# Key latents normed before they are halved, keys taken out by ScalarE, and short products set between long ones

## The chip, the cores and the metric

The kernel runs on one core of a Trainium2 chip. Its engines are TensorE (PE in the profile, with its weight loads as PEld), VectorE (DVE), ScalarE (ACT), GpSimd (POOL) and SyncE (SP), which here issues every DMA. Each engine runs its own instructions strictly in the order in which they were written, and waits on semaphores. The metric is the device time of one execution in microseconds, as the median of several.

## What is computed

Two transformer blocks on 512 tokens of width 1024, all in float32 with the token axis along the free dimension. The second block, where the change lies, has two attentions side by side:

```python
h = rmsnorm_2(x, norm_g[l])
(q_lat, c_kv, k_rope, z_a, q_b, k_b, v_b, z_b,
 q_idx, k_idx, w_idx, gate_a, gate_b) = jnp.split(h @ w_in[l], cuts, axis=-1)
q = (rmsnorm_2(q_lat, g_q_lat[l]) @ w_uq[l])      # 384 latents -> 8 heads of 96
kv = (rmsnorm_2(c_kv, g_kv_lat[l]) @ w_ukv[l])    # 256 latents -> 8 heads of 64 keys + 64 values
...
y_a = mla_attention(q_nope, q_pe, k_nope, k_pe, v_a, pos) * silu(z_a)
y_b = dsa_attention(q_b, k_b, v_b, q_idx, k_idx, w_idx, rel_bias, pos, topk) * silu(z_b)
merged = sigmoid(gate_a) * (y_a @ w_o_a[l]) + sigmoid(gate_b) * (y_b @ w_o_b[l])
x = x + merged @ w_out[l]
```

The second attention (dsa) first scores all keys with eight small index heads, keeps the 128 best keys of each query, and masks the rest.

## The kernel before

**Products.** Every product of float32 matrices is made of three passes: each operand is split in a high half, a rounded copy that ScalarE makes, and a low half, the remainder that VectorE or GpSimd subtracts (`HH`/`HL` for the normed input, `LQH`/`LQL` for the query latents, `LKH`/`LKL` for the key latents, `WH`/`WL` for weights). The three matmuls of a tile are lines 1352 to 1354, of 512 columns each. Weights come in units of 8 tiles: SyncE loads a unit into `WS` (L1235) once the low half of the unit three before it is made, ScalarE makes `WH` (L1537), GpSimd in this part of the program makes `WL` (L2115), and a unit is asked for two units ahead of its use. A `product` of eight tiles thus takes 24 matmuls in four quarters of six, and ends in a take-out of its PSUM bank. Products use bank 0 and bank 1 in turn (`d_ring`), so a product can start only when the take-out of the product but one before it is done.

**Order.** Nothing is scheduled at run time. Python generators write one list of steps; `weave` takes one step of the main work and then so many of the side work, a product giving way after each quarter, and every engine follows the list.

**Index stage.** The main work is `index_scores` (24 index products, L1502, into four banks in turn; ScalarE turns each into `i_t`, L1731; VectorE adds it into `score`, L2026 and L2029). The 24 come as three blocks of eight heads, for 512, 384 and 256 columns. The side work is `latents`, then `mla_v`, then `mla_products(0)`:
- `latents` makes the key latents `ckv0`, `ckv1` and the query latents `ql0` to `ql2`. A latent (`lat_out`) is taken out by VectorE into a buffer `tmp` (L2049), squared by ScalarE (L1545), added up by GpSimd into `acc` (L2163), split by ScalarE (L1735) and VectorE (L2054). The sums over the partitions are matmuls with ones (L1383, and L1389 for the same sums token by token). After `ql0` the key sums are turned into the norm `RK` and, token by token, into `rtok` (step `norm_kv`: Ln, Ln, Exp, Exp with two table loads, L1739 to L1747). After three quarters of `za0`, the first gate product, the query sums follow, and `norm_q` makes `RQ` (L1750 to L2058).
- `mla_v` is the value product, four token blocks of twelve short matmuls (L1376 to L1378), taken out by ScalarE with the scale `rtok` into `a_v` (L1563).
- `mla_products(p)` is, for a pair of heads, the key product `uk` (2 tiles), the two query products `uq` (3 tiles each) and, past the first pair, `za` (8 tiles). VectorE takes the keys out times `RK` (step `mla_k`, L2062, two instructions of 64 rows) and the queries times `RQ` (`mla_q`, L2065).

**Attention stage.** The main work is the attention of eight mla heads and then eight dsa heads. Per head it has four blocks: logits (L1456, or L1461 to L1467 for dsa), row maximum on VectorE (L1922, or L1926 for dsa), exponential on ScalarE (L1635), scaling by the inverse sum (L1640 on ScalarE, for dsa L1937 on VectorE), transposes (L1475) and the product with the values (L1484). The side work is `mla_side`, which holds the remaining products in a fixed order. VectorE also finds the 128 best keys in 48 rounds of two scans (L2038, L2040). Each dsa head needs stacked halves of its queries and keys (`dsa_stack`); four DMAs for a pair of heads (L1283, L1288) move rows, and stand in SyncE's queue between the weight loads.

## Time and profile before

| | us |
|---|---|
| median of 3 runs | 1107.36 |
| range of the runs | 1106.17 to 1107.45 |
| the profiled execution, its own time | 1106.37 |
| its span in the profile | 1104.6 |
| PE busy in it | 1050.1 |
| DVE / ACT / POOL busy | 623.3 / 469.3 / 256.6 |

The span is the time from the first to the last recorded instruction of the profiled execution. PE is busy for 95% of it; what a change can gain or lose is mostly found in PE's remaining 54.5 us, each of them a wait for another engine or for a DMA. In the timeline a row gives the start and the duration of an instruction or of several merged ones, and in brackets how long the engine stood idle before it and on whom it waited.

### The profile page before, as it was taken

To read this page: it belongs to the slowest core of one execution; us is meant where nothing else is said; L and a number is where in the kernel's file an instruction comes from. 1 tells how busy PE (TensorE), PEld (TensorE's weight loads), DVE (VectorE), ACT (ScalarE), POOL (GpSimd) and SP (SyncE) were. 2 spreads that over 40 slices of the span, in tenths; PEclk is the share of its full clock that TensorE was granted. 3 is DMA by queue.
4 is the path that set the end of the run, shared out by engine and by line. 5 is a ranking of instruction groups with operands and counts; after the bars stand their busy time and mean duration, and the time that the engine had idled before them with its cause. 6 is when DMAs were issued, how large, how long until landed. Compare 5 with 4: busy or idle time off the path is not lost.

```text
span 1104.6 us, 13494 instructions
## 1 busy us (share of the span) xinstructions
PE 1050.1 (95%) x5160; PEld 843.1 (76%) x5160; DVE 623.3 (56%) x1048; ACT 469.3 (42%) x815; POOL 256.6 (23%) x155
## 2 busy tenths in 40 slices
PE   7799889899999999999999998799999999999996
PEld 5597677667888888888888776577787766788885
DVE  6755577747454433344444556898756665425544
ACT  6634346546322222132334465545764554423322
POOL 0581332222101000011113323422323223321100
PEclk9999899999999999999999999999999999999998
DMA  8031132212223232223233326212222423122222
GB/s 293 4 122 50 39 117 78 78 58 77 96 96 96 98 131 77 94 83 109 93 100 94 110 70 209 85 39 74 60 88 78 118 91 104 59 96 96 99 73 77
DMA packets 34655, 102.32 MB, mean 93 GB/s; under 512 B 4544, under 2 KB 8016, under 8 KB 34592
## 3 DMA queue, kind: packets, MB, share of 16 engines
q1 hardware_dynamic: 34592, 101.47, 28.3%
q8 instruction: 41, 0.67, 0.3%
q14 instruction: 22, 0.18, 0.1%
HBM read 93.35 MB, written 4.74 MB: 89 GB/s over the span
## 4 chain that ended last, share of the span: by engine, by line
PE 73%; DVE 14%; ACT 6%; issue 4%; SPq 2%; DMA 1%; DVEq 0%; POOL 0%; ACTq 0%; POOLq 0%
PE bank L1352 20%; PE bank L1354 20%; PE bank L1353 20%; PE bank L1484 2%; PE bank L1475 2%; PE bank L1364 1%; DVE m L2038 1%; DVE score L2029 1%; PE bank L1366 1%; PE bank L1365 1%; DVE score L2040 1%; ACT WH L1537 1%; DVE f_s L1828 1%; DVE small L1922 1%; PE bank L1456 1%
## 5 line engine op out<-in xcount | busy, mean ns | idle before, releaser
L1352 PE MATMUL bank<-HH,WH 128*128 128x512 f32 x808 | 330.1, 409 | 16.9 <-DVE WL L1784 8.3
L1354 PE MATMUL bank<-HH,WL 128*128 128x512 f32 x808 | 317.8, 393 | 0.0
L1353 PE MATMUL bank<-HL,WH 128*128 128x512 f32 x808 | 317.4, 393 | 0.0
L2115 POOL TENSOR_TENSOR WL<-WS,WH 128x1024 fp32r<-128x1024 f32 x64 | 154.8, 2419 | 358.1 <-ACT WH L1537 357.7
L1352 PEld LDWEIGHTS bank<-HH,WH 128*128 128x128 f32 x808 | 154.2, 191 | 54.4 <-DVE WL L1784 8.3
L1537 ACT ACTIVATE WH<-WS 128x1024 fp32r<-128x1024 f32 x162 | 168.6, 1047 | 56.5 <-PE bank L1354 41.5
L1354 PEld LDWEIGHTS bank<-HH,WL 128*128 128x128 f32 x808 | 153.1, 189 | 33.4
L1353 PEld LDWEIGHTS bank<-HL,WH 128*128 128x128 f32 x808 | 153.8, 190 | 29.5 <-issue 1.0
L1784 DVE TENSOR_TENSOR WL<-WS,WH 128x1024 fp32r<-128x1024 f32 x98 | 130.3, 1335 | 25.9 <-ACT WH L1537 25.9
L2168 POOL TENSOR_TENSOR fa<-fa,fg 128x512 f32<-128x512 f32 x22 | 28.3, 1285 | 273.4 <-DVE fa L1975 273.4
L1352 PE MATMUL bank<-GH,WH 128*128 128x512 f32 x176 | 68.5, 389 | 0.0
L1353 PE MATMUL bank<-GL,WH 128*128 128x512 f32 x176 | 68.5, 389 | 0.0
L1354 PE MATMUL bank<-GH,WL 128*128 128x512 f32 x176 | 68.5, 389 | 0.0
L1955 DVE TENSOR_TENSOR X<-X,bank 128x512 f32<-128x512 f32 x39 | 26.7, 685 | 67.9 <-PE bank L1354 67.8
L1680 ACT ACTIVATE GH<-fa 128x512 fp32r<-128x512 f32 x22 | 13.9, 632 | 114.3 <-POOL fa L2168 114.3
L1545 ACT ACTIVATE sq<-X 128x512 f32<-128x512 f32 x31 | 19.5, 629 | 74.5 <-DVE X L1955 74.2
L1364 PE MATMUL bank<-WH,HH 128*128 128x256 f32 x160 | 47.2, 295 | 2.0 <-ACT f_v L1563 2.0
L1648 ACT ACTIVATE PT<-bank 128x128 f32<-128x128 f32 (+1 forms) x96 | 41.1, 428 | 16.1 <-PE bank L1475 15.9
L1366 PE MATMUL bank<-WH,HL 128*128 128x256 f32 x160 | 45.2, 283 | 0.0
L1365 PE MATMUL bank<-WL,HH 128*128 128x256 f32 x160 | 45.2, 283 | 0.0
L1977 DVE TENSOR_TENSOR GL<-fa,GH 128x512 fp32r<-128x512 f32 x22 | 15.2, 692 | 46.8 <-ACT GH L1680 46.8
L1676 ACT ACTIVATE fs<-fg 128x512 f32<-128x512 f32 x22 | 13.9, 632 | 59.6 <-DVE fg L1966 59.6
(339 smaller groups left out, 1749.7 us busy)
## 6 DMA issues: line engine op xcount, KB each, us to landing
WS<-wall SPq DMA_DIRECT2D x162, 512.0 KB, 3.4
scratch<-rows SPq DMA_DIRECT2D x8, 320.0 KB, 5.6
X<-xT SPq DMA_DIRECT2D x8, 256.0 KB, 6.2
b_t<-scratch SPq DMA_DIRECT2D x8, 256.0 KB, 3.8
outT<-X SPq DMA_DIRECT2D x8, 256.0 KB, 2.1
b_m<-b_m SPq DMA_DIRECT2D x11, 128.0 KB, 4.1
f_s<-f_s SPq DMA_DIRECT2D x8, 128.0 KB
f_m<-f_m SPq DMA_DIRECT2D x8, 128.0 KB
```

What stands on the lines that cost most here:

```text
L1352: e.matmul(b[:, :], wh, xh[:, at_k, :], start=k == 0, stop=False)
L1353: e.matmul(b[:, :], wh, xl[:, at_k, :], start=False, stop=False)
L1354: m = e.matmul(b[:, :], wl, xh[:, at_k, :], start=False, stop=k == n - 1)
L1364: e.matmul(b[:, 0:256], xh[:, k, cs], wh, start=k == 0, stop=False)
L1365: e.matmul(b[:, 0:256], xh[:, k, cs], wl, start=False, stop=False)
L1366: m = e.matmul(b[:, 0:256], xl[:, k, cs], wh, start=False, stop=k == NK - 1)
L1537: e.activation(WH[:, u % NW, :], WS[:, u % NST, :], ACT.Copy).then_inc(*w_hi.tick(u))
L1648: e.activation(dst, s["b"][:, 0:128 * i + 128].rearrange("p (a n) -> p a n", n=128), ACT.Copy).then_inc(*moved.tick(s["u"]))
L1784: e.tensor_tensor(WL[:, u % NW, :], WS[:, u % NST, :], f32(WH[:, u % NW, :]), ALU.subtract).then_inc(*w_low_v.tick(u))
L1955: e.tensor_tensor(X[:, m, :], X[:, m, :], s["b"][:, :], ALU.add).then_inc(*out_v.tick(s["name"]))
L2115: e.tensor_tensor(WL[:, u % NW, :], WS[:, u % NST, :], f32(WH[:, u % NW, :]), ALU.subtract).then_inc(*tick(w_low_g, u))
L2168: e.tensor_tensor(a[:, :], a[:, :], fg[jj % 3][:, :], ALU.mult).then_inc(*tick(gate_up, jj))
```

## The change

It has five parts.
- **Latents of the keys.** `ckv0` and `ckv1` are taken out into `a_q[2]` and `a_q[3]`. They are not split at once: after `ql2` two new VectorE steps multiply them by `RK` (`norm_latent`), and only then they are split.
- **Sums.** The key sums and `norm_kv` stand after `ql1` and not after `ql0`. The token-by-token sums (four matmuls with one column) and their two small activations are gone, since the values no longer need a scale.
- **Keys.** The keys are taken out by ScalarE with a plain copy, not by VectorE; the logits wait for ScalarE as well.
- **Order in the first pair.** The four blocks of the value product alternate with `uk0`, `uq0` and `uq1`.
- **Order in the attention stage.** `mla_side` puts `za`, a part of `dsa_products(0)` or a gate product between the short `uk` and `uq` products. The gate product `gate_a(1)` moves for that from the dsa part to the mla part.

```diff
@@ lat_out
+                if x == "lk":
+                    do("latent", c=c, x=x, name=name, b=b, t=a_q[2 + c], free=None)
+                    add_square((x, c), total_g, a_q[2 + c][:, :], None, out_v(name))
+                    return out_v(name)
@@ latents
-                if c == 0:
+                if c == 1:
                     i1, b1 = column_sums("lk", acc[1], total_g(("lk", 1)))
-                    i2, b2 = token_sums("lkt", [acc[1]], total_g(("lk", 1)))
-                    do("norm_kv", b1=b1, b2=b2)
+                    do("norm_kv", b1=b1)
                     t_ring.give(i1, norm_a("lk ln"))
-                    t_ring.give(i2, norm_a("lkt ln"))
+                if c == 2:
+                    for c2 in range(2):
+                        do("norm_latent", c=c2, t=a_q[2 + c2])
+                        do("halve_latent", c=c2, x="lk", t=a_q[2 + c2])
+                        known.add(("lk", c2))
@@ the first pair
+        def first_pair():
+            values = mla_v()
+            for part in (mla_key(0), lambda: mla_query(0, 0), lambda: mla_query(0, 1)):
+                next(values)
+                yield
+                yield from part() if callable(part) else part
+            yield from values
@@
-        side = chain(latents(), mla_v(), mla_products(0))
+        side = chain(latents(), first_pair())
@@ mla_side
-            yield from mla_products(1)
-            yield from dsa_products(0)
-            yield from mla_products(2)
-            yield from gate_a(0)
-            yield from mla_products(3)
+            yield from mla_key(1)
+            yield from z_products("za", P_ZA, 1)
+            yield from mla_query(1, 0)
+            yield from dsa_query(0)
+            yield from mla_query(1, 1)
+            yield from dsa_key(0)
+            for p in range(2, 4):
+                yield from mla_key(p)
+                yield from gate_a(p - 2)
+                yield from mla_query(p, 0)
+                yield from z_products("za", P_ZA, p)
+                yield from mla_query(p, 1)
...
-            yield from gate_a(1)
@@ scalar_program
+                elif kind == "mla_k":
+                    r = slice(64 * s["hl"], 64 * s["hl"] + 64)
+                    q.wait_ge(dense(f"uk{s['p']}"), s["free"])
+                    e.activation(s["dst"][0:64, :], s["b"][r, :], ACT.Copy).then_inc(*out_a.tick(s["name"]))
@@ vector_program
-                elif kind == "mla_k":
...
+                elif kind == "norm_latent":
+                    q.wait_ge(norm_a("lk"), square(("lk", s["c"])))
+                    e.tensor_tensor(s["t"][:, :], s["t"][:, :], RK[:, :], ALU.mult).then_inc(*norm_v.tick(("lk", s["c"])))
```

Three places show how the order moves. The first is ScalarE's queue around `norm_kv` (`RK` and `rtok`). Before, it stood behind the last `i_t` of `ql0`'s stretch and ahead of the split `WH` and the `i_t` of head 4 of the first block:

```order
L1731 ACTIVATE i_t3_159<-bank7 128x512
L1739 ACT_TABLE_LOAD
L1739 ACTIVATE RK_214<-bank5,eps_61 128x512
L1742 ACTIVATE rtok_64<-bank4,eps_61 128x4
L1745 ACT_TABLE_LOAD
L1745 ACTIVATE RK_214<-RK_214 128x512
L1747 ACTIVATE rtok_64<-rtok_64 128x4
L1537 ACTIVATE WH_53<-WS_52 128x1024
L1731 ACTIVATE i_t0_156<-bank2 128x512
```

Now it stands behind the last `i_t` of the first block and ahead of the next split and of the first `i_t` of the second block (384 columns). The seven instructions between the two places (a split, four `i_t`, a square and a split of a latent) are as before.

```order
L1766 ACTIVATE LQH_162<-tmp1_70,V_60 128x512
L1762 ACTIVATE i_t3_159<-bank7 128x512
L1770 ACT_TABLE_LOAD
L1770 ACTIVATE RK_214<-bank5,eps_61 128x512
L1773 ACT_TABLE_LOAD
L1773 ACTIVATE RK_214<-RK_214 128x512
L1568 ACTIVATE WH_53<-WS_52 128x1024
L1762 ACTIVATE i_t0_156<-bank2 128x384
L1762 ACTIVATE i_t1_157<-bank6 128x384
```

The second place is one product further on, after `ql2`. ScalarE has before, ahead of `RQ`:

```order
L1545 ACTIVATE sq1_68<-tmp0_69 128x512
L1735 ACTIVATE LQH_162<-tmp0_69,V_60 128x512
L1731 ACTIVATE i_t3_159<-bank7 128x384
L1537 ACTIVATE WH_53<-WS_52 128x1024
L1731 ACTIVATE i_t0_156<-bank2 128x384
L1731 ACTIVATE i_t1_157<-bank6 128x384
L1750 ACT_TABLE_LOAD
L1750 ACTIVATE RQ_213<-bank5,eps_61 128x512
```

and now the two splits of the key latents, each of which waits for VectorE's multiplication, stand ahead of `WH`:

```order
L1576 ACTIVATE sq1_68<-tmp0_69 128x512
L1766 ACTIVATE LQH_162<-tmp0_69,V_60 128x512
L1762 ACTIVATE i_t3_159<-bank7 128x384
L1766 ACTIVATE LKH_164<-a_q2_187,V_60 128x512
L1766 ACTIVATE LKH_164<-a_q3_188,V_60 128x512
L1568 ACTIVATE WH_53<-WS_52 128x1024
L1762 ACTIVATE i_t0_156<-bank2 128x384
L1762 ACTIVATE i_t1_157<-bank6 128x384
L1780 ACT_TABLE_LOAD
L1780 ACTIVATE RQ_213<-bank4,eps_61 128x512
```

VectorE's queue at that place, now; before, the third row was followed at once by the fourth and the ninth:

```order
L2059 SCALAR_TENSOR_TENSOR score_160<-i_t2_158,wi_72,score_160 128x384
L2079 TENSOR_TENSOR tmp0_69<-bank0,Rb_62 128x512
L2084 SCALAR_TENSOR_TENSOR LQL_163<-tmp0_69,V_60,LQH_162 128x512
L2059 SCALAR_TENSOR_TENSOR score_160<-i_t3_159,wi_72,score_160 128x384
L2091 TENSOR_TENSOR a_q2_187<-a_q2_187,RK_214 128x512
L2084 SCALAR_TENSOR_TENSOR LKL_165<-a_q2_187,V_60,LKH_164 128x512
L2091 TENSOR_TENSOR a_q3_188<-a_q3_188,RK_214 128x512
L2084 SCALAR_TENSOR_TENSOR LKL_165<-a_q3_188,V_60,LKH_164 128x512
L2059 SCALAR_TENSOR_TENSOR score_160<-i_t0_156,wi_72,score_160 128x384
```

Four instructions more are on VectorE between the query latent and the next scores (the two `LKL` splits stood earlier before). The third place is TensorE's queue after the first block of the value product and the first index product of the third block (256 columns). Before, the second value block followed, in bank 1:

```order
L1378 MATMUL bank0<-WH_53,LKL_165 128x256
L1502 MATMUL bank2<-i_kk_145,i_qq0_148 128x256
L1376 MATMUL bank1<-WH_53,LKH_164 128x256
L1377 MATMUL bank1<-WL_54,LKH_164 128x256
L1378 MATMUL bank1<-WH_53,LKL_165 128x256
```

Now the first pair's key product stands there, also in bank 1:

```order
L1409 MATMUL bank0<-WH_53,LKL_165 128x256
L1533 MATMUL bank2<-i_kk_145,i_qq0_148 128x256
L1383 MATMUL bank1<-LKH_164,WH_53 128x512
L1384 MATMUL bank1<-LKL_165,WH_53 128x512
L1385 MATMUL bank1<-LKH_164,WL_54 128x512
```

Bank 1 holds `za0` until its take-out in both.

## Rows read from the trace of the kernel before

**Rows 1.** Part 1 of the page: busy us, share of the span, instructions.
```profile
PE 1050.1 (95%) x5160; PEld 843.1 (76%) x5160; DVE 623.3 (56%) x1048; ACT 469.3 (42%) x815; POOL 256.6 (23%) x155
```

**Rows 2.** Whom TensorE waited for, 640 to 800 us: total, times, longest.
```profile
PE bank L1383 <- POOL acc L2163: 4.4, 1, 4.4
PE bank L1352 <- DVE a_q L2065: 4.3, 2, 3.1
PE bank L1376 <- DVE zb L1801: 1.6, 1, 1.6
PE bank L1475 <- ACT Pc L1640: 1.0, 1, 1.0
...
PE bank L1376 <- ACT a_v L1563: 0.4, 1, 0.4
```

**Rows 3.** The same view, 720 to 1000 us.
```profile
PE bank L1461 <- issue: 2.2, 1, 2.2
PE bank L1461 <- DVE sq_late L2001: 1.7, 1, 1.7
```

**Rows 4.** TensorE's timeline: start, duration, what, idle time before.
```profile
667.22 1.02 PE L1383 MATMUL bank<-acc,ones 128*128 128x512 f32 x2
668.08 0.95 PE L1389 MATMUL bank<-ones,acc 128*128 128x1 f32 x8
...
682.53 0.44 PE L1502 MATMUL bank<-i_kk,i_qq 96*128 96x384 f32 x1 [0.74 <-ACT i_t L1731]
...
691.84 2.07 PE L1383 MATMUL bank<-acc,ones 128*128 128x512 f32 x2 [4.39 <-POOL acc L2163]
...
699.45 0.39 PE L1376 MATMUL bank<-WH,LKH 128*128 128x256 f32 x1 [1.65 <-DVE zb L1801]
...
716.96 0.50 PE L1352 MATMUL bank<-LQH,WH 128*128 128x512 f32 x1 [3.07 <-DVE a_q L2065]
```

**Rows 5.** Chain of work: the weight load that ScalarE waits for.
```profile
670.36 3.87 DMA WS<-wall
```

**Rows 6.** ScalarE's timeline.
```profile
669.65 1.28 ACT L1739 ACT_TABLE_LOAD   x1
...
673.64 0.19 ACT L1747 ACTIVATE rtok<-rtok 128x4 f32<-128x4 f32 x1
674.25 1.06 ACT L1537 ACTIVATE WH<-WS 128x1024 fp32r<-128x1024 f32 x1 [0.42 <-DMA WS<-wall]
...
683.32 1.24 ACT L1731 ACTIVATE i_t<-bank 128x384 f32<-128x384 f32 x3
...
690.29 0.71 ACT L1735 ACTIVATE LQH<-tmp,V 128x512 fp32r<-128x512 f32 x1
...
691.27 1.04 ACT L1537 ACTIVATE WH<-WS 128x1024 fp32r<-128x1024 f32 x1
...
696.39 0.63 ACT L1753 ACTIVATE RQ<-RQ 128x512 f32<-128x512 f32 x1
...
880.13 0.62 ACT L1713 ACTIVATE b_s<-b_st 64x512 fp32r<-64x512 f32 x1
```

**Rows 7.** VectorE's timeline.
```profile
675.82 4.29 DVE L2029 SCALAR_TENSOR_TENSOR score<-i_t,wi,score 128x512 f32<-128x512 f32 x3 [5.22 <-ACT i_t L1731]
...
684.11 2.37 DVE L2026 TENSOR_SCALAR score<-i_t,wi 128x384 f32<-128x384 f32 x1
...
689.04 0.68 DVE L2049 TENSOR_TENSOR tmp<-bank,Rb 128x512 f32<-128x512 f32 x1
...
691.03 1.31 DVE L2054 SCALAR_TENSOR_TENSOR LQL<-tmp,V,LQH 128x512 fp32r<-128x512 f32 x1 [1.31 <-ACT LQH L1735]
...
698.71 0.68 DVE L1801 SCALAR_TENSOR_TENSOR zb<-bank,Rb 128x512 f32<-128x512 f32 x1
```

**Rows 8.** GpSimd's timeline: one low half of a weight unit.
```profile
683.57 2.69 POOL L2115 TENSOR_TENSOR WL<-WS,WH 128x1024 fp32r<-128x1024 f32 x1 [0.78 <-ACT WH L1537]
```

**Rows 9.** 692 to 696 us: length, PE, PEld, DVE, ACT, POOL busy, clock, DMA share, GB/s.
```profile
692.00:696.00 4.00, 4.00 (x10) 2.60 (x11) 3.90 (x4) 3.95 (x6) 2.63 (x1) 0.61 0.00 0
```

**Rows 10.** SyncE's timeline around the DMAs of head 6.
```profile
913.58 5.54 SPq L1235 DMA_DIRECT2D WS<-wall  x2
919.17 0.47 SPq L1283 DMA_DIRECT2D b_m<-b_m  x1
919.68 0.59 SPq L1288 DMA_DIRECT2D b_m<-b_m  x1
```

More of the change, by code:

```diff
@@ L937, in out @@
                 add_square((x, c), total_g, t[:, :], None, out_v(name))
-                do("halve_latent", c=c, x=x, t=t, name=name)
+                do("halve_latent", c=c, x=x, t=t)
                 tmp_ring.give(m, low((x, c)))
@@ L977, in mla_v @@
                 do("mm_av", tb=tb, tiles=tiles, b=b, free=free)
-                do("out_tok", name="av", tb=tb, dst=a_v[:, tb, :], b=b, scale=rtok[:, 4 + tb:5 + tb],
-                   norm=norm_a("lkt"), free=[index_in[0](), index_in[1]()])
+                do("out_tok", name="av", tb=tb, dst=a_v[:, tb, :], b=b, scale=1.0, norm=None,
+                   free=[index_in[0](), index_in[1]()])
                 d_ring.give(i, out_a(("av", tb)))
@@ L995, in z_products, with mla_key @@
             gates[name] = i, z
-        def mla_products(p):
+        slots_of = {}
+        def mla_key(p):
             while not aq_ring.ready(2):
                 yield "not yet"
-            slots = [aq_ring.take() for _ in range(2)]
+            slots = slots_of[p] = [aq_ring.take() for _ in range(2)]
             def k_out(b):
@@ L1004, in k_out, with mla_query, out @@
                     do("mla_k", name=(f"uk{p}", hl), hl=hl, dst=a_k[slots[hl][0]], p=p, b=b, free=slots[hl][2])
-                return out_v((f"uk{p}", 1))
-            def q_out(hd, hl):
-                def out(b):
-                    do("mla_q", name=f"uq{hd}", dst=a_q[slots[hl][0]], b=b, free=slots[hl][2])
-                    known.add(f"uq{hd}")
-                    return out_v(f"uq{hd}")
-                return out
-            yield from product(f"uk{p}", "w_ukv_2", 0, cols(256 * p, 64) + cols(256 * p + 128, 64), "lk", 2, k_out)
-            for hl in range(2):
-                hd = 2 * p + hl
-                yield from product(f"uq{hd}", "w_uq_2", 0, cols(96 * hd, 96) + cols(96 * hd + 80, 16)
-                                   + cols(96 * hd + 64, 16), "lq", 3, q_out(hd, hl))
-            if p:
-                yield from z_products("za", P_ZA, p)
-            mla_in[p] = slots
+                return out_a((f"uk{p}", 1))
+            yield from product(f"uk{p}", "w_ukv_2", 0, cols(256 * p, 64) + cols(256 * p + 128, 64), "lk", 2, k_out)
+        def mla_query(p, hl):
+            hd, slot = 2 * p + hl, slots_of[p][hl]
+            def out(b):
+                do("mla_q", name=f"uq{hd}", dst=a_q[slot[0]], b=b, free=slot[2])
+                known.add(f"uq{hd}")
+                return out_v(f"uq{hd}")
+            yield from product(f"uq{hd}", "w_uq_2", 0, cols(96 * hd, 96) + cols(96 * hd + 80, 16)
+                               + cols(96 * hd + 64, 16), "lq", 3, out)
+            if hl:
+                mla_in[p] = slots_of[p]
+        def first_pair():
[5 more added lines that the diff above has]
+            yield from values
         def mla_pair(p):
@@ L1086, in dsa_stack, with dsa_query @@
                 yield
-        def dsa_products(p):
+        dsa_free = {}
+        def dsa_query(p):
             while (p == 1 and ("logits", ("mla", 5, 3)) not in known) or (p == 2 and ("logits", ("mla", 7, 3)) not in known) \
@@ L1099, in dsa_products @@
             first.append(dsa_stack(p))
+        def dsa_products(p):
+            yield from dsa_query(p)
+            yield from dsa_key(p)
         def dsa_pair(p):
@@ L1454, in tensor_program @@
                     elif kind == "logits_mla":
-                        q.wait_ge(out_v(f"uq{hd}"), rope("end"), keys_in(), s["free"])
+                        q.wait_ge(out_v(f"uq{hd}"), out_a((f"uk{hd // 2}", hl)), rope("end"), keys_in(), s["free"])
                         e.matmul(b[:, 0:n], s["qk"][0][:, qs], s["qk"][1][:, 0:n], start=True, stop=False)
```

16 lines of the change are left out of this document (5 added, 11 removed).

## The prediction

> **What bounds the kernel now.** The first view is the page's part 1: TensorE is busy 1050.1 us of a span of 1104.6 [rows 1], so it is the bound, and a change counts by how it shortens TensorE's work or its waits. The second is the table of TensorE's waits. In the stretch that the change rewrites it lists one wait of 4.4 us for GpSimd's sum of squares, 4.3 us for two query take-outs, 1.6 and 0.4 us in the value product and 1.0 us in the attention [rows 2]; behind it 2.2 and 1.7 us at the first logits of two dsa heads [rows 3]. The third is the timeline of each engine, which says what stands behind such a wait. The 4.39 us ahead of 691.84 [rows 4] end with a GpSimd addition, but that is the end of a chain: VectorE takes `ql2` out at 689.04, because it was busy with scores before that, and one score there lasted 2.37 us [rows 7], while GpSimd held a weight split from 683.57 for 2.69 us [rows 8]. ScalarE then needs 0.71 us for each split copy [rows 6]. So between 667 and 717 us the small engines, with their queues in fixed order, set the pace, and what counts there is which instruction stands ahead of which. A loss comes on top: after the 4.39 us the granted clock is 0.61 over the next 4 us [rows 9], part of them at the lower level of 1.2 GHz; the stretch shows what a long wait costs beyond itself.
>
> **The change part by part.** All times are those of the profiled execution; I follow the queues with its durations.
>
> *Sums, TensorE's side.* The token sums go: from 668.08 to the next product at about 668.9 [rows 4] is 0.8 us, and `ql1` starts 1.7 us earlier since the other sums now follow it. This is worth nothing yet. ScalarE's split at 674.25 waits for a weight load that SyncE issued at 670.36 [rows 5, 6], behind DMAs the change leaves alone. VectorE's three scores start at 675.82 behind it [rows 7], `ql1` is taken out after them, and the index product at 682.53 waits for the `i_t` at the end of that chain [rows 4]. TensorE arrives there 0.8 us earlier and waits 0.8 us longer: 0.
>
> *`norm_kv`, ScalarE's side.* Before, it ran from 669.65 to 673.83 [rows 6], in time in which ScalarE would have waited for that load anyway: it cost nothing. Now the cover is gone. It stands at 682.4, ahead of a weight split and the first `i_t` of the second block. Without the two small activations it is two table loads of 1.28 us, an Ln of 0.7 and an Exp of 0.6, 3.9 us. That `i_t`, the first of three from 683.32 [rows 6], ends at 687.7, and the score that ran at 684.11 [rows 7] starts then: **+3.6**. Everything queued behind it on VectorE shifts with it: the take-out of `ql2` to 692.7, the query sums on TensorE from 691.84 to 695.5. Meanwhile TensorE waits at index product 4 of the second block for the same `i_t` (about 3.6 us) and at the sums again (about 4.6). The two are one delay of 3.6 over the wait of before.
>
> *Latents normed late.* One latent costs a multiplication (0.65), ScalarE's copy (0.71), VectorE's remainder (0.7), none overlapping the next, since each engine waits for the other. The nearest row is the query latent, where VectorE stands 1.31 us for ScalarE and its own part then takes 1.31 against GpSimd [rows 7]. After `LQL` at 696.0 and a score, the first key latent is ready at 698.7, the second at 700.7. TensorE reaches the value product at 699.6 and waits about a microsecond for the second. That is small. What matters is who is queued behind: ScalarE's `WH`, before at 691.27 [rows 6], stands behind both splits and starts at 699.9, **+8.6**. From there to the end of `RQ` it is 691.27 to 697.0, 5.75 us [rows 6]: `RQ` is ready at 705.65. VectorE then has its `RQ` product, a score and the take-out of `za0`, which ends at 707.6; before it ran at 698.71 [rows 7]. `za0` holds bank 1. TensorE has by then done the first value block and one index product, and waits for bank 1 from 702 on; before it continued at 699.45 [rows 4]. It is **8.2 us late** at 707.6.
>
> *The first pair.* From 699.45 to 716.96 [rows 4] TensorE did the other three value blocks, `uk0`, `uq0`, `uq1`, `uk1` and seven index products. Without its waits (0.4 and 4.3 [rows 2]) that is 17.5 - 4.7 = 12.8 us, and the same work stands there now, in another order. The long waits for `uq` take-outs go, as the value blocks stand between. New ones come: ScalarE has, after 707.6, a tanh, a split, a value take-out, an `i_t`, a second split, and only then the two keys (priced at the 64-row copy of 0.62 [rows 6]), so `uq0` starts at 712.2, about a microsecond late; two GpSimd splits in a row slow the scores ahead of `uq0`'s take-out, so `uq1` starts at 717.4, 1.3 us late; and the clock after the wait for bank 1 falls as in [rows 9], partly hidden in these waits. `uk1` ends at 722.65 where before it was over by 716.96: **+5.7** so far. Bounds: 3 (the new waits do not occur) to 9 (they each cost a score under GpSimd, 2.4, more).
>
> *Keys on ScalarE.* Eight instructions of some 0.7 us leave VectorE, which is full in the attention's first 30 us. The logits' new wait is met long before, as other products stand between. Of the 1.0 us wait of the transposes [rows 2] and two of 0.2 next to it I take 0.7 as gained; bounds 0 and 1.3, and 2 lost if ScalarE, with keys ahead of an exponential, becomes late instead. **-0.7**.
>
> *`gate_a(1)` moved.* It leaves the dsa part, so the last query and key products come 5.6 us of TensorE's time earlier. Head 6's DMAs were issued at 919.17 and 919.68 behind a weight load that SyncE held until 919.1 [rows 10], and its logits waited 2.2 us [rows 3]. In the new order one weight load fewer stands between and the stack is made one block of the attention, some 3.5 us, earlier: the wait goes, **-2.2**. Head 4's wait of 1.7 [rows 3] keeps its order, but its weight split stands behind one more PT copy: **+0.5**. Elsewhere in that part the same instructions stand in nearly the same order.
>
> Sum: 5.7 - 0.7 - 2.2 + 0.5 = **+3.3 us**. On the profiled execution this is 1106.37 + 3.3 = 1109.7. That execution is 1.0 us below the median, whose runs spread over 1.3; on the median it is 1107.36 + 3.3 = 1110.7, which I forecast.
>
> The scores that stretch under GpSimd's splits are a term of this sum. The row of 2.37 us against 0.6 shows it. The Trainium skill (SBUF — State Buffer, the section on ports) gives the rule: VectorE with two inputs in SBUF and GpSimd hold one port pair in turn, each for a whole instruction, so the one that starts first wins. By that rule the new multiplications by `RK` can also be held up, by up to one split; in my timing they fall between two splits. A second place speaks harder against the change: the Trainium skill (ScalarE: Activation LUTs, What ACT_TABLE_LOAD costs) prices a table switch at about 2.66 us with a drain. The row has 1.28 us, and two loads with all four activations fit between 669.65 and 673.83 [rows 6]. By the page's figure the sum would be 2.8 us higher; I go by the row.
>
> **The rivals.**
> *A: the change does what its parts suggest.* `norm_kv` and the late norm find cover, since ScalarE is only 42% busy [rows 1]; then the token sums' 0.8, the waits of 4.3 and 0.4, the 1.0 and the 2.2 go, 8.7 us together: 1098.7. For it speaks the idle time of ScalarE in the stretch. Against it: that idle time lies where ScalarE waits for VectorE to take a latent out, and the new place is between two such waits, right where VectorE's next score hangs on ScalarE. The point from which it decides is 684.11: if the score of that row starts before 685, A is right.
> *B: slower at first, given back later.* The delay up to `uk1` is there but nearer its lower bound of 3 us, and the attention, relieved on VectorE, and the two dsa heads give back 3.9: within 1 us of before, 1107.
> *C: the small engines stay late.* VectorE reaches the attention with its scans still to do, and ScalarE has the keys besides; two or three more waits of 1 to 2 us in the attention, and clock drops after each long wait: 3.3 + 5 = 1115.7.
> *D: the new order does not reach the waits.* If bank waits and not the queues decided, the interleaving would change nothing past 0.8 us: 1106.6. The rows give each wait a queue, so this is weak, and is counted with B.
>
> **How the numbers follow.** Forecast 0.52, A 0.15, B and D 0.20, C 0.13. A measurement tells 0.2%, 2.2 us, from no change. Forecast and C, less the edge of the forecast below +2.2 (0.07), give slower 0.58; that edge and most of B give same 0.24; A and a little of B give faster 0.18. The range leaves out the far part of A and the far part of C: from 1102.5, a gain of half of A, to 1115. The likeliest case's own range is 1108.5 to 1113.5.
>
> **What would show it.** Right, in the profile of after: the first score of the second block near 687.7 and not 684; TensorE waiting at an index product of 384 columns for `i_t` for over 3 us, then at the query sums for over 4; a wait of some 5 us of `uk0` for `za0`'s take-out near 707; the waits for `a_q` below 1.5 us each; no wait at head 6's first logits. It would be wrong if `norm_kv` ran in ScalarE's idle time, if the value product waited longer for the key latents than for bank 1, or if the time lost by 720 us were not there at 850.

## The result, and the profile after

The changed kernel takes 1118.57 us (median of 4 runs, 1115.30 to 1123.89), the kernel before 1107.40 beside it. The ratio is 1.0102, with a 95% interval of 1.0074 to 1.0130: **slower by 11.2 us**, where the prediction had +3.3 and at most +7.6. The profiled execution of it took 1115.54 us with a span of 1113.8, near the lowest of the runs, and its span is 9.2 us longer than the span of before.

Part 1 of the page after, to be read beside [rows 1]. TensorE's busy time is only 2.4 us longer, so most of the loss is waiting. A pass that runs at the lower clock counts as busy time:

```profile
PE 1052.5 (95%) x5144; PEld 845.0 (76%) x5152; DVE 620.7 (56%) x1042; ACT 474.0 (43%) x821; POOL 256.5 (23%) x155
```

Whom TensorE waited for, 640 to 800 us, against [rows 2] (total, times, longest; product matmuls are line 1383, value products 1407, sums 1414, index products 1533, transposes 1506):

```profile
PE bank L1533 <- ACT i_t L1762: 5.0, 2, 3.4
PE bank L1383 <- DVE zb L1831: 4.5, 1, 4.5
PE bank L1383 <- DVE a_q L2094: 2.5, 2, 1.2
PE bank L1407 <- DVE LKL L2084: 1.9, 2, 1.5
PE bank L1506 <- ACT Pc L1671: 1.6, 3, 0.7
PE bank L1414 <- POOL acc L2192: 1.5, 1, 1.5
```

The same view from 720 to 1000 us, against [rows 3]:

```profile
PE bank L1506 <- DVE Pc L1967: 3.6, 1, 3.6
PE bank L1492 <- issue: 2.2, 1, 2.2
```

The wait for `i_t` is there as forecast, the wait for `za0`'s take-out too. Head 6's 2.2 us is still there, and a wait of 3.6 us that no row of before has stands at 899 us.

**A ledger for all kernels.** Time positions of two kernels with different orders can't be compared directly, since one may have done more of the side work by then. So I read, in each trace, when TensorE starts the logits of a head (they come in the same order in every kernel). I took off the shift that the trace has already just ahead of the index stage (at the product matmul at 647.83 before, 644.93 after, the same program up to there), and 0.232 us, the spacing of two product matmuls at full clock, for each product matmul that the kernel has done more than the one before. What is left is what has been lost since 640 us. The columns are: the first logits of the attention (end of the index stage), the first dsa head (end of the mla part), the third block of dsa head 4, and the last logits of the attention. The ratio is to the kernel before as timed beside that kernel (its medians were 1107.2 to 1108.5), so two rows are better compared by their ratios than by their medians. Each ledger comes from one execution and holds what the clock lost in it: up to the attention side_new does the work of before in its order, and still its first column is 1.7.

| kernel | median us, runs | ratio to before, 95% | index stage | mla part | head 4 | end |
|---|---|---|---|---|---|---|
| changed | 1118.57, 4 | 1.0102 (1.0074 to 1.0130) | 5.6 | 8.7 | 12.1 | 12.0 |
| changed, once more | 1117.75, 4 | 1.0094 (1.0065 to 1.0123) | 5.5 | 8.5 | 12.1 | 12.2 |
| side_new | 1113.58, 5 | 1.0052 (1.0031 to 1.0072) | 1.7 | 4.7 | 8.2 | 10.0 |
| side_old | 1114.60, 4 | 1.0058 (1.0035 to 1.0081) | 5.5 | 5.5 | 5.7 | 7.3 |
| gate_back | 1120.83, 4 | 1.0118 (1.0096 to 1.0139) | 5.6 | 9.5 | 12.5 | 16.1 |
| norm_early | 1113.81, 5 | 1.0058 (1.0036 to 1.0079) | 1.5 | 4.6 | 9.9 | 9.8 |
| early_split | 1107.91, 10 | 0.9990 (0.9973 to 1.0006) | -1.1 | -1.1 | -0.9 | 0.7 |
| early_old | 1108.17, 10 | 0.9984 (0.9963 to 1.0005) | -1.2 | -1.2 | -1.1 | -1.1 |
| ya_ahead | 1114.93, 7 | 1.0055 (1.0034 to 1.0077) | 5.7 | 8.7 | 9.4 | 8.5 |
| head_old | 1117.17, 4 | 1.0085 (1.0058 to 1.0111) | 5.9 | 6.9 | 12.4 | 12.6 |
| row_early | 1111.19, 7 | 1.0029 (1.0009 to 1.0048) | 3.8 | 3.8 | 5.7 | 7.3 |
| gate_between | 1104.21, 10 | 0.9966 (0.9952 to 0.9980) | -1.2 | -1.2 | -3.3 | -1.4 |
| za_first | 1122.13, 4 | 1.0142 (1.0109 to 1.0176) | 5.6 | 13.9 | 15.3 | 15.1 |

For the changed kernel it reads: 5.6 us lost in the index stage, 3.1 in the mla part, 3.4 ahead of dsa head 4, nothing after. That is 12.0 to 12.1, of which the profiled execution shows 9.2, as it came to the index stage 2.9 us early. That lead is the clock and not the change, as the section on the hardware shows.

### The profile page after: what moved, and what is told of

The parts are those of the page before. It is cut to its first block, busy times and chain, and to the rows that moved or that the text cites. A ratio compares the mean times of both kernels' runs of the same rounds, so it can differ in the third digit from the quotient of the medians.

```text
span 1113.8 us, 13461 instructions
## 1 busy us (share of the span) xinstructions
PE 1052.5 (95%) x5144; PEld 845.0 (76%) x5152; DVE 620.7 (56%) x1042; ACT 474.0 (43%) x821; POOL 256.5 (23%) x155
## 4 chain that ended last, share of the span: by engine, by line
PE 74%; DVE 13%; ACT 6%; issue 3%; SPq 2%; DMA 1%; DVEq 0%; POOL 0%; ACTq 0%; POOLq 0%
PE bank L1383 20%; PE bank L1385 20%; PE bank L1384 20%; PE bank L1515 2%; PE bank L1506 2%; PE bank L1395 2%; PE bank L1397 1%; PE bank L1396 1%; ACT WH L1568 1%; DVE m L2068 1%; DVE score L2059 1%; DVE score L2070 1%; DVE f_s L1858 1%; PE bank L1487 1%; DVE small L1952 1%
## 5 line engine op out<-in xcount | busy, mean ns | idle before, releaser
L1711 ACT ACTIVATE GH<-fa 128x512 fp32r<-128x512 f32 x22 | 13.9, 634 | 114.3 <-POOL fa L2197 114.3
L1707 ACT ACTIVATE fs<-fg 128x512 f32<-128x512 f32 x22 | 13.9, 634 | 59.5 <-DVE fg L1996 59.5
```

## The experiments

Each is described as an edit of the changed kernel unless its text says otherwise. In the diffs, - is the kernel edited.

### Which stretch loses for which reason: side_new, side_old

side_new is the kernel before with the new order in the attention stage alone (with the key and query products split into `mla_key` and `mla_query`, keys still taken out by VectorE). side_old is the changed kernel with the old order there:

```diff
@@ mla_side, side_old
             yield from mla_key(1)
-            yield from z_products("za", P_ZA, 1)
             yield from mla_query(1, 0)
-            yield from dsa_query(0)
             yield from mla_query(1, 1)
+            yield from z_products("za", P_ZA, 1)
+            yield from dsa_query(0)
             yield from dsa_key(0)
...
             yield from z_products("zb", P_ZB, 2)
+            yield from gate_a(1)
             yield from dsa_products(3)
```

> The kernel before, with only the new order in the attention stage (short uk and uq products between long ones, gate_a(1) moved to the mla part). The index stage, the norms, and VectorE's key take-outs are those of before. Against before: if each stretch loses for its own reason (theory 1), the wait of some 3.6 us at the turns ahead of dsa head 4 is here too, head 6's wait of 2.2 stays, and the attention adds 1 to 3 us of waits: +4 to +6 us. If the attention and the dsa part lose only because the index stage ends late (theory 2), nothing is lost here: -2.2 to +1 us.

> The changed kernel with the old order in the attention stage; what is left of the change is the index stage (late norm, late latents, value blocks between the first pair's products) and the keys taken out by ScalarE. Theory 1 (each stretch has its own loss): the index stage's 5.7 us stay and the attention adds at most 1, the dsa part nothing: +5 to +7 us against before. Theory 2 (what is late in the index stage is late further on): waits in the attention and at dsa head 4 come as in the changed kernel, +9 to +12 us.

Measured: +0.52% and +0.58%, 5.8 and 6.4 us. **Theory 1 holds, and the parts add up.** side_new loses 3.0 us in the mla part and 3.5 ahead of head 4, as the changed kernel does (3.1 and 3.4), though it enters the attention 3.9 us earlier. side_old carries its 5.5 us from the index stage through the mla part unchanged, to the tenth. So neither the late index stage nor the keys on ScalarE cost or gain anything further on in these traces; the order of the side work loses 6.5 us by itself. The 1.7 us of side_new in the index stage are mostly a clock drop: its waits there are no longer than before (1.19 and 3.06 us for the query take-outs), but soon behind the second one the passes stand 0.43 us apart, where before they stood 0.23 apart (717.30, 717.53, 717.76) behind a wait of 3.07 [rows 4]. TensorE's timeline of side_new:

```profile
713.76 0.50 PE L1367 MATMUL bank<-HH,WH 128*128 128x512 f32 x1 [3.06 <-DVE a_q L2080]
...
715.88 0.63 PE L1367 MATMUL bank<-HH,WH 128*128 128x512 f32 x1
716.31 0.63 PE L1368 MATMUL bank<-HL,WH 128*128 128x512 f32 x1
```

### The index stage: norm_early, early_split, early_old, row_early

norm_early puts the key sums and `norm_kv` back behind `ql0`:

```diff
-                if c == 1:
+                if c == 0:
                     i1, b1 = column_sums("lk", acc[1], total_g(("lk", 1)))
                     do("norm_kv", b1=b1)
```

> The changed kernel with the key sums and norm_kv back behind ql0; the latents are still normed and split after ql2. Theory 1 (norm_kv in front of the second block's first i_t costs 3.6 us of the 5.7): the waits for i_t of 1.5 and 3.4 us go, the sums wait up to 4.4 again for GpSimd, and the wait of uk0 for za0 stays: 2 to 4 us less than the changed kernel. Theory 2 (the late latents alone set the pace of the index stage): uk0 starts at the same time and at most 0.5 us is won.

Measured: 4.8 us less than the changed kernel by the medians, 4.1 by the ledger's first column (5.6 against 1.5). Theory 1: the place of `norm_kv` costs 4.1 us. The wait for `i_t` of 3.4 us is gone (one of 1.2 stays), the sums wait 4.4 again, and `uk0` waits 5.5 for `za0`, for the latents are still late. Summed up to the first logits the waits of the stage are 12.4 us against 14.1; the rest of the 4.1 is the lower clock between them.

early_split and early_old build on side_old with that edit, and move the norm and the splits of the latents as well; early_old is:

```diff
-                if c == 2:
-                    for c2 in range(2):
-                        do("norm_latent", c=c2, t=a_q[2 + c2])
+                if c == 0:
+                    for c2 in range(2):
+                        do("norm_latent", c=c2, t=a_q[2 + c2])
+                    for c2 in range(2):
                         do("halve_latent", c=c2, x="lk", t=a_q[2 + c2])
```

> The changed kernel with the old order in the attention stage, with the key sums and norm_kv back behind ql0, and with the latents normed there; the first is split there too, the second behind ql1. The value blocks still stand between the first pair's products, the token sums stay gone and ScalarE takes the keys out. Theory 1 (what was lost in the index stage came only from where norm_kv and the late latents stand, and the interleaving itself wins most of the 4.3 us of take-out waits): uk0 waits under 2 us, uq0 and uq1 under 1 each, the index stage ends 2 to 4 us earlier than before: -2 to -4 us against before. Theory 2 (the interleaving wins nothing, since each first-pair product then stands behind another wait): within 1 us of before.

> As early_split, but both key latents are split at once behind norm_kv. Two ScalarE copies of 0.7 us then stand ahead of the weight split of 674.25 and of the first block's scores. Theory 1: some 0.7 us slower than early_split, as the scores of 675.8 hang on that split. Theory 2 (there is slack before the i_t wait at 682.5): the same as early_split within 0.3 us, or faster, since nothing is in front of the second block.

Measured: 0.9990 and 0.9984, neither apart from 1. The ledger has -1.1 and -1.2 us for the index stage, so norming and splitting the latents late cost 2.7 us (norm_early's 1.5 against -1.2). The two kernels can't be told apart: that the second latent is split later does not show, so theory 2 of early_old. By its time early_split came out where its theory 2 had put it, within 1 us of before; row_early will show that theory 2's reason, an interleaving that wins nothing, is not the one, so theory 1 had the mechanism and not the size. `uq1` still waits 1.3 us, `uk0` 1.6 in early_old, and the waits for `i_t` are 1.1 and 1.7 us where before had a single one of 0.7, as the norm's steps now stand ahead of the first block's scores. TensorE's waits of early_old, 640 to 800 us:

```profile
PE bank L1419 <- POOL acc L2197: 4.4, 1, 4.4
PE bank L1538 <- ACT i_t L1767: 2.8, 2, 1.7
PE bank L1388 <- DVE zb L1836: 1.6, 1, 1.6
PE bank L1388 <- DVE a_q L2099: 1.3, 1, 1.3
```

row_early is early_old with the value blocks in a row again:

```diff
-        side = chain(latents(), first_pair())
+        side = chain(latents(), mla_v(), mla_key(0), mla_query(0, 0), mla_query(0, 1))
```

> early_old with the four value blocks in a row ahead of the first pair's products, as in the kernel before; it tells what the interleaving alone is worth. Theory 1 (the value blocks between the short products take up the take-out waits): without them uq0 waits 1.2 and uq1 3.1 us again as before, and the time is 2 to 3 us above early_old. Theory 2 (it only moves waits): within 0.7 us of early_old.

Measured: 1111.19, 3.0 us above early_old by the medians, 0.45% or 5.0 us by the ratios and 5.0 by the ledger. Theory 1: the query take-outs cost 4.2 us again. Value blocks between the short products are worth 3 to 5 us, the one part of the change that is shown to win. The waits up to the first logits are 2.1 us longer in sum (13.1 against 11.0); the rest of the ledger's 5.0 is clock. row_early shows a second thing. It has everything of the new index stage but the interleaving, with the norm and the latents early, and it loses 3.8 us to before there (ratio 1.0029, interval 1.0009 to 1.0048). So these steps are not free when they stand early either: early_old is level with before since the interleaving pays for them. Its waits in the same stretch:

```profile
PE bank L1388 <- DVE a_q L2099: 4.2, 2, 3.3
PE bank L1412 <- DVE zb L1836: 3.2, 1, 3.2
PE bank L1538 <- ACT i_t L1767: 2.8, 2, 1.7
```

### The mla part: head_old, za_first

```diff
@@ head_old
             yield from mla_key(1)
-            yield from z_products("za", P_ZA, 1)
             yield from mla_query(1, 0)
-            yield from dsa_query(0)
             yield from mla_query(1, 1)
+            yield from z_products("za", P_ZA, 1)
+            yield from dsa_query(0)
             yield from dsa_key(0)
@@ za_first
                 yield from mla_key(p)
-                yield from gate_a(p - 2)
+                yield from z_products("za", P_ZA, p)
                 yield from mla_query(p, 0)
-                yield from z_products("za", P_ZA, p)
+                yield from gate_a(p - 2)
                 yield from mla_query(p, 1)
```

> The changed kernel with the first part of the attention's side work in the old order (uk1, uq2, uq3, za1, qb0, kb0), the rest as changed. Theory 1 (the 3 us that the new order loses in the attention come from what stands between in its first 30 us, where VectorE is full): the waits for Pc of 0.3, 0.6, 0.2 and 0.7 us fall back to one of about 1.0 and the 0.5 for b_st goes, so 1 to 2 us are won; the 1.2 us wait for a_q at 780 stays. Theory 2 (they come from the keys on ScalarE or from the late index stage): nothing is won.

> The changed kernel with za(p) behind uk(p) and the gate product between the two uq products of the pair, for pairs 2 and 3: za and gate have changed places. Theory 1 (the 1.2 us wait near 780 is uq5's take-out, which stands on VectorE behind the wait for za2's tanh): the wait falls below 0.5. Theory 2 (it is the short product itself, uk3 behind uq5, that leaves no time for any take-out): it stays at about 1.2. The sum moves by at most 1.5 us.

head_old: the mla part loses 1.0 us in place of 3.1, and the waits for `Pc` fall back to one of 0.9; theory 1. The median is only 1.4 us lower, which the intervals of the ratios don't tell apart, since it loses 5.5 us ahead of head 4 in place of 3.4 (its two waits there are 3.36 and 1.78 us). The changed kernel's timelines show what stands ahead of the waits. `za1` now ends in the attention's first head. VectorE takes it out and then waits 1.51 us for its tanh, and the multiplication behind it runs beside a low half on GpSimd from 728.30 and takes 2.55 us; before, it waited 1.04 us for the tanh and took 0.69 at 733.21, with no low half beside it. Behind it on VectorE stand a round of the two scans and then the reciprocal that ScalarE's scaling of `Pc` waits for, and TensorE's transposes wait for that. What the wait for the tanh and what the overlap with GpSimd costs, no run separates. VectorE, ScalarE, GpSimd, TensorE:

```profile
728.71 2.55 DVE L1835 SCALAR_TENSOR_TENSOR zb<-tmp,zb 128x512 f32<-128x512 f32 x1 [1.51 <-ACT tmp L1590]
...
732.56 0.15 DVE L1964 RECIPROCAL small<-small 128x1 f32<-128x1 f32 x1
```

```profile
732.75 0.51 ACT L1671 ACTIVATE Pc<-Pc,small 128x256 f32<-128x256 f32 x1 [4.08 <-DVE small L1964]
```

```profile
728.30 2.41 POOL L2144 TENSOR_TENSOR WL<-WS,WH 128x1024 fp32r<-128x1024 f32 x1 [5.58 <-ACT WH L1568]
```

```profile
733.31 0.44 PE L1506 MATMUL bank<-ident,Pc 128*128 128x128 f32 x2 [0.28 <-ACT Pc L1671]
...
737.46 0.55 PE L1506 MATMUL bank<-ident,Pc 128*128 128x128 f32 x3 [0.59 <-ACT Pc L1671]
...
741.12 0.66 PE L1506 MATMUL bank<-ident,Pc 128*128 128x128 f32 x4 [0.72 <-ACT Pc L1671]
```

za_first: neither theory as written. In the changed kernel the product behind `uk3`, a gate product, waits 1.24 us for `uq5`'s take-out, with `uk3` alone (1.4 us of TensorE's work) to cover it. Here that wait is gone, and a new one of 1.28 us stands one product earlier: `uk3` itself waits for the take-out of the gate product, although the nine passes of `uq5`, 2.1 us, lie between. TensorE and VectorE of za_first:

```profile
784.56 0.50 PE L1383 MATMUL bank<-LKH,WH 128*128 128x512 f32 x1 [1.28 <-DVE acc L2098]
```

```profile
783.83 0.68 DVE L2098 SCALAR_TENSOR_TENSOR acc<-bank,Rb 128x512 f32<-128x512 f32 x1
```

Both take-outs start late after the last pass of their product: 2.6 us here (781.2 to 783.83), 2.4 in the changed kernel (777.15 to 779.55). Here VectorE makes scans and row maxima without a pause until then. In the changed kernel it stood idle 1.26 us for the tanh up to 777.15, when the product ended, and then had the multiplication behind the tanh, a round of scans and a row maximum ahead of the take-out. So the tanh may well be a part of the wait there, but a wait of the same size comes without one, from VectorE's other work ahead of the take-out. That the short `uk3` is to blame is not shown either: the next product behind it starts only at 793.60 here, too late to wait for anything.

The time of za_first is 3.6 us above the changed kernel, where I had expected at most 1.5 either way. The ledger has the loss in the third to the fifth head. The planner (the Python code that writes the list of steps) had to finish pair 2's products in one go between the fourth and the fifth head (774.93 to 786.06 without logits), and the transposes and value products of these heads were left with less cover, one of them waiting 2.78 us. That the one led to the other is my reading of the order; no run tests it.

### Ahead of dsa head 4: gate_back, ya_ahead, gate_between

```diff
@@ gate_back
-                yield from gate_a(p - 2)
+                if p == 2:
+                    yield from gate_a(0)
...
             yield from z_products("zb", P_ZB, 2)
+            yield from gate_a(1)
             yield from dsa_products(3)
@@ ya_ahead
             yield from z_products("zb", P_ZB, 2)
+            yield from gated_ya(1)
             yield from dsa_products(3)
-            yield from gated_ya(1)
@@ gate_between, an edit of early_old
             yield from dsa_products(2)
+            yield from gate_a(1)
             yield from z_products("zb", P_ZB, 2)
-            yield from gate_a(1)
             yield from dsa_products(3)
```

> The changed kernel with the gate product gate_a(1) back in the dsa part, behind zb2; all else is as changed. If its 24 matmuls were the cover of VectorE's chain of stacks and scalings ahead of dsa head 4 (theory 1), the wait of 3.6 us there shrinks to below 1: about 3 us less than the changed kernel. If the wait comes from what is late before it, or from the stacks and GpSimd alone (theory 2), it stays and the time is that of the changed kernel within 1 us.

> The changed kernel with gated_ya(1) ahead of dsa_products(3) in the side work, and nothing else. In the changed kernel the planner asks for dsa_products(3) before the stack of the pair before it is planned, and two turns of the side work pass with no product, so TensorE has fewer products in the head ahead of dsa head 4; here it has one quarter more there (6 matmuls, 1.4 us). Theory 1 (the wait of 3.6 us at the turn is that missing cover, with a clock drop behind it): the waits of 3.6 and 0.6 shrink to about 2.5 in sum and 1.5 to 3.5 us are won against the changed kernel. Theory 2 (the chain of stacks is late for another reason): the waits stay above 4 in sum and nothing is won.

> early_old with gate_a(1) between dsa_products(2) and zb2, where it stood behind zb2 before. 24 matmuls more (5.6 us) then lie between kb2 and the first logits of dsa head 4. Theory 1 (cover decides at head 4): its wait of 1.8 us goes, the wait of 2.3 us at head 6 stays: 1.5 to 2 us less than early_old, 2 to 4 less than before. Theory 2 (the stacks follow the take-outs wherever those stand, and the chain gets a new wait): within 0.7 us of early_old.

First the place in the changed kernel. VectorE makes the stacks of head 4 there; one of its steps waits for ScalarE, then runs beside a low half on GpSimd and takes 2.35 us, and the scaling `Pc`, on which TensorE's transposes wait, stands behind it. VectorE, GpSimd, TensorE:

```profile
896.60 2.35 DVE L2028 TENSOR_TENSOR b_s<-b_st,b_s 64x512 fp32r<-64x512 f32 x1 [2.16 <-ACT b_s L1744]
...
899.18 0.35 DVE L1967 TENSOR_SCALAR Pc<-Pc,small 128x256 f32<-128x256 f32 x1
```

```profile
896.06 2.34 POOL L2144 TENSOR_TENSOR WL<-WS,WH 128x1024 fp32r<-128x1024 f32 x1 [5.72 <-ACT WH L1568]
```

```profile
895.24 0.27 PE L1506 MATMUL bank<-ident,Pc 128*128 128x128 f32 x1
...
895.58 0.40 PE L1493 MATMUL bank<-b_m,b_s 128*128 128x512 f32 x1
899.59 0.69 PE L1506 MATMUL bank<-ident,Pc 128*128 128x128 f32 x2 [3.61 <-DVE Pc L1967]
...
900.50 0.63 PE L1384 MATMUL bank<-HL,WH 128*128 128x512 f32 x1
```

The chain is there before as well: the same VectorE step stood at 884.78 and took 2.40. But between the two transposes TensorE then had two quarters of a product, twelve passes of 0.232 us each, and waited 0.19 us; now it has none. From the take-out of `kb2` to the first logits of head 4 TensorE waits 4.2 us in sum now (3.61 and 0.64) and 1.9 before (0.19 and 1.74 [rows 3]). Behind the wait the six passes up to 902.7 run mostly at the lower clock, 0.43 us apart (granted clock 0.57 from 899 to 903 us), which costs some 1.2 us, about the rest of the 3.4.

gate_back: neither theory as written. The wait at the transposes is gone, but head 4's logits now wait 3.36 us for their rows, which a DMA had still to bring, and head 6's logits 4.43 in place of 2.2; it ends 2.3 us above the changed kernel. Its ledger still loses 3.0 us between the first dsa head and head 4 (9.5 to 12.5). Bringing the product back to the dsa part did not bring back the order of before, as the other side work had moved too, so the loss at head 4 is not the gate product's move alone. ya_ahead: theory 1, with two quarters more ahead of head 4, where I had counted one. Its waits there are 0.65, 0.84 and 0.88 us, 2.4 in sum, with no clock drop behind them, and the time is 3.6 us below the changed kernel. The wait of head 6 is gone in it as well, in exchange for 0.86 and 1.1 us at transposes and value products. gate_between: theory 1. With two quarters more than early_old ahead of head 4, no wait over 0.2 us is left there (-1.2 to -3.3 in the ledger), and head 6's stays, here with a clock drop behind it that takes the last column back to -1.4. Against early_old the ratios alone decide nothing, as their intervals overlap; the missing wait does:

```profile
PE bank L1497 <- issue: 2.2, 1, 2.2
PE bank L1511 <- ACT Pc L1676: 0.9, 1, 0.9
PE bank L1511 <- DVE Pc L1972: 0.2, 1, 0.2
```

**gate_between beats both kernels**: 1104.21 us, 0.34% below before (interval 0.20 to 0.48%) and 1.3% below the changed kernel. It keeps of the change the norm ahead of the split, without the token sums, the keys on ScalarE and the interleaved value blocks; the norm and the latents stand early, and the attention's side work is in the old order but for `gate_a(1)`.

### The same program again: after_again

> The changed kernel once more, unchanged, to see which of its lower clock stretches come in each execution. If the drops hang on the program alone, the same stretches show the same granted clock (0.70 in 680:690, 0.84 in 690:700, 0.60 in 700:710, 0.96 in 120:160) and the ledger reads the same within 0.3 us. If they hang on the moment of the waits as well, single stretches differ by 1 to 3 us while the waits themselves are the same.

The index stage, the mla part and head 4 give the ledger of the first run within 0.2 us; the waits agree within 0.2 us too. The spans differ by 2.3 us, 2.2 of it before 640 us. The profile shows both kinds of behaviour: the drops behind the index stage's waits come each time, and those of the early part move.

## Why the prediction was right or wrong

**The result against the sum.** Of the four terms the first was right: +5.7 for the index stage, measured 5.6. The other three were wrong: -0.7 came out as 0, -2.2 as 0 and +0.5 as +3.4. And the new order in the mla part, which had no term, cost 3.1.

**Index stage, +5.7: right (5.6), in nearly all its steps.** Taking off the 2.9 us of lead, the first score of the second block was to start at 684.8 and did at 684.66; `ql2`'s take-out was to start at 689.8 and did at 689.53; the query sums at 692.6, measured 692.33; `za0`'s take-out was to end at 704.7, and `uk0` started at 704.69, after a wait of 4.48 us. VectorE, changed kernel:

```profile
684.66 2.31 DVE L2056 TENSOR_SCALAR score<-i_t,wi 128x384 f32<-128x384 f32 x1 [3.60 <-ACT i_t L1762]
...
689.53 0.68 DVE L2079 TENSOR_TENSOR tmp<-bank,Rb 128x512 f32<-128x512 f32 x1
...
703.95 0.69 DVE L1831 SCALAR_TENSOR_TENSOR zb<-bank,Rb 128x512 f32<-128x512 f32 x1
```

norm_early and early_old confirm that both moves lose: 4.1 us for `norm_kv` (3.6 in the prediction) and 2.7 for the late latents. The multiplications by `RK` took 0.68 and 0.69 us and were not held up, as forecast. One sign was off: the sums waited 1.5 us and not over 4. TensorE arrived there late because it ran its products at the lower clock between the waits (0.70 from 680 to 690 us), so the time was lost in another column. The microsecond of waiting that the prediction gave `uq0` did not come either: `uq0` started at 709.32 without a wait, as the six passes of `uk0` took 2.9 us at the lower clock in place of 1.55. That the two came to the same start is luck. The waits from 640 to 720 us are 14.4 us in sum and were 11.7, only 2.7 more; the rest of the 5.6 is the clock. The prediction had the clock only as a part of its bounds, partly hidden in the waits, so the hit to 0.1 us is in part luck; in the other traces with the whole new index stage it is 5.5 to 5.9. ScalarE's norm took 3.84 us (679.37 to 683.21) with two table loads of 1.28, so the row decides against the 2.66 us of the Trainium skill (ScalarE: Activation LUTs, What ACT_TABLE_LOAD costs) here:

```profile
679.37 1.28 ACT L1770 ACT_TABLE_LOAD   x1
680.67 0.69 ACT L1770 ACTIVATE RK<-bank,eps 128x512 f32<-128x512 f32 x1
681.38 1.28 ACT L1773 ACT_TABLE_LOAD   x1
682.67 0.63 ACT L1773 ACTIVATE RK<-RK 128x512 f32<-128x512 f32 x1
683.21 1.04 ACT L1568 ACTIVATE WH<-WS 128x1024 fp32r<-128x1024 f32 x1
```

**Keys on ScalarE, -0.7: wrong, 0.0.** side_old has 5.5 us at both ends of the mla part, and its wait at the transposes is 0.92 us where before it was 0.98 (the 1.0 of [rows 2]). The wait is the tail of a chain over `za1`'s take-out; VectorE's two key instructions are not in it.

**The order in the mla part: the step that was missing, +3.1.** The prediction gave the new order no term of its own. It argued that the logits' wait is met early "as other products stand between", which is TensorE's side. On VectorE's side the new order puts long take-outs with a tanh into the heads in which VectorE is full. Of the 3.1, head_old shows 2.1 for the part up to `kb0`. The waits account for 2.2 (3.5 now, 1.3 before). The other 0.9 lie in TensorE's busy time, at full clock and with no idle time listed; what they are stays open.

**`gate_a(1)` moved, -2.2 and +0.5: wrong, 0 and +3.4.** The step that failed is "elsewhere in that part the same instructions stand in nearly the same order". They do, but the head ahead of head 4 has two quarters of a product less, and a wait of 3.61 us stands where before had 0.19. By the order of the steps the planner asked for `qb3` before the stack ahead of it was planned and passed over its turns; ya_ahead, which puts another product into these turns, wins 2.7 us there. gate_back shows that the gate product's move is not the whole of it. At head 6 SyncE issued the rows at 928.35, again straight behind a weight load that it had held until 927.98, as in [rows 10]; one load fewer in the queue did not bring that one forward. SyncE, changed kernel:

```profile
927.98 0.33 SPq L1266 DMA_DIRECT2D WS<-wall  x1
928.35 0.47 SPq L1314 DMA_DIRECT2D b_m<-b_m  x1
```

**The rivals.** C, the small engines stay late, came nearest in the sum (1115.7) but for another reason: lateness was not handed on, as side_old shows, each stretch made its own. A fell at its own decision point: the score started at 684.66 plus the 2.9 of lead, 687.6, and not before 685. The range missed because its upper end, +7.6 us, held one further mishap. The change had two, one in a place without a term and one in a part that I had priced at a gain.

## What to carry to other kernels

- A norm or a split that ran while its engine waited for a load is free only there. Moved by one product it cost 4.1 us, and multiplications ahead of a split, each of which waits for the other engine, 2.7 us. The same instructions early cost less, but they were not free: row_early still loses 3.8 us in the stage.
- Short products between long ones win (3 to 5 us here) where the long ones need little of the small engines, as value blocks do. Where the long one ends in a take-out, a tanh and a second pass over the data, it lost 2.1 us (head_old).
- When side work is moved out of a stretch, look at each chain of small-engine steps in that stretch and count the products that TensorE has beside it, in the order of the new kernel. Two quarters of a product more or less decided 2 to 3 us.

## What the runs showed of the hardware

The granted clock is a chance term of some microseconds in each execution. Up to 640 us all these kernels are the same program, but their drops to the lower level of 1.2 GHz are not the same. The kernel before ran the stretch 124 to 132 us at 0.64 and 0.51; the changed one ran it at full clock, and the later stretch from 152 to 160 us at 0.87 and 0.70, where before had 1.00 in both. The windows (length, PE, PEld, DVE, ACT, POOL busy, clock, DMA share, GB/s), before:

```profile
124.00:128.00 4.00, 4.00 (x26) 2.92 (x25) 0.00 (x0) 0.00 (x0) 0.00 (x0) 0.64 0.00 0
128.00:132.00 4.00, 4.00 (x12) 2.90 (x11) 0.75 (x1) 1.88 (x2) 2.07 (x4) 0.51 0.00 0
152.00:156.00 4.00, 3.30 (x27) 2.91 (x26) 3.48 (x5) 0.99 (x3) 2.54 (x1) 1.00 0.46 147
```

and after:

```profile
124.00:128.00 4.00, 4.00 (x30) 3.13 (x29) 0.58 (x1) 1.19 (x2) 1.05 (x2) 1.00 0.00 0
128.00:132.00 4.00, 4.00 (x17) 2.93 (x16) 0.35 (x2) 3.57 (x5) 1.03 (x2) 1.00 0.00 0
152.00:156.00 4.00, 2.13 (x13) 2.13 (x14) 2.55 (x5) 2.40 (x6) 0.00 (x0) 0.87 0.49 160
156.00:160.00 4.00, 4.00 (x20) 3.30 (x20) 2.73 (x8) 1.73 (x5) 0.00 (x0) 0.70 0.46 109
```

These two stretches are the 2.9 us of lead: at one and the same product pass the changed kernel is 0.2 us ahead at 12 us, 3.4 at 132 and 2.9 from 162 on. In the index stage the drops of the changed kernel are heavier, between waits that follow each other closely (length, PE busy, clock among the columns):

```profile
680.00:690.00 10.00, 6.56 (x19) 5.03 (x18) 6.19 (x10) 5.35 (x8) 2.36 (x1) 0.70 0.43 154
690.00:700.00 10.00, 6.54 (x25) 4.50 (x24) 6.53 (x8) 6.17 (x10) 3.31 (x2) 0.84 0.17 48
700.00:710.00 10.00, 5.52 (x24) 4.65 (x24) 8.22 (x13) 8.53 (x15) 3.86 (x3) 0.60 0.19 59
```

A wait of 2.1 to 2.5 us at dsa head 6 brought a drop of some 1.6 us in side_new, side_old, early_split, row_early and gate_between, and none in the kernel before, both runs of the changed kernel, early_old, norm_early, head_old and za_first. So a single profiled execution tells the waits to a tenth or two, but the time of a kernel only to several us; early_old's ten runs stand in two groups, at 1102.0 to 1102.7 and at 1108.1 to 1109.6. What decides whether a given wait brings a drop stays open.
